# Side work of TensorE moved to common ticks in a two-block language model on one core

## What is computed

```python
# first block
x = x + mamba2_mixer(x, ...)        # 32 heads of 64 in 4 groups, state 128, chunks of 128 tokens
x = x + conv_ffn(x, ...)            # gate and up of 2816, 3-tap convolution, silu
k, v = shared_kv(x, ...)
x = x + diff_attention(x, k, v, ...)  # 8 heads, two softmaxes each, p0 - lam * p1
x = x + conv_ffn(x, ...)
# second block
h = rms_norm(x)
y_conv, y_fox, y_swa = ...          # short convolution; forgetting attention, 8 heads of 64;
                                    # window attention of 128 tokens with sinks, 8 heads, 2 kv heads
x = x + (g0 * (y_conv @ w0) + g1 * (y_fox @ w1) + g2 * (y_swa @ w2)) @ w_mix_out
x = x + cross_attention(rms_norm(x), rms_norm(mem), ...)   # 4 heads of 256, 256 memory tokens
x = x + swiglu(rms_norm(x), ...)
out = rms_norm(x)
```

## Time and profile before

| what | value |
|---|---|
| median of three runs | 2459.2 us (2458.94 to 2461.61) |
| profiled execution | 2459.41 us |
| its span, first to last instruction | 2457.6 us |
| TensorE busy | 2418.4 us, 98% |
| VectorE, ScalarE, POOL busy | 1398.4, 972.2, 406.3 us |
| DMA engines busy | 27.2% (weights), 2.0%, 0.3% by queue |
| mean granted clock of TensorE | 0.995 |

### The profile page before, as it was taken

How to read it: one execution, slowest core, us unless ns; L and a number is a source line. 1 busy time by engine, 2 the same in 40 slices (tenths; PEclk the granted TensorE clock), 3 DMA queues, 4 the chain that set the end, 5 groups by cost and what they waited for, 6 DMA issues and landing times.

```text
span 2457.6 us, 30359 instructions
## 1 busy us (share of the span) xinstructions
PE 2418.4 (98%) x11930; PEld 1963.1 (80%) x11930; DVE 1398.4 (57%) x2286; ACT 972.2 (40%) x1595; POOL 406.3 (17%) x320
## 2 busy tenths in 40 slices
PE   8899999999999999999999999999999999999998
PEld 6677777888888887878888887787788887888887
DVE  6878876663665445576546547534565445343342
ACT  5444434442344444454334434424443334322223
POOL 0352332220111222122002100001220101110011
PEclk9999999999999999999999999999999999999999
DMA  4532222223223221132232242231234322223222
GB/s 160 101 88 86 78 69 77 95 94 102 96 84 122 65 69 51 48 113 97 90 105 91 81 137 78 69 112 53 65 120 134 120 87 85 98 91 102 96 84 87
DMA packets 74269, 226.23 MB, mean 92 GB/s; under 512 B 8080, under 2 KB 12304, under 8 KB 74000
## 3 DMA queue, kind: packets, MB, share of 16 engines
q1 hardware_dynamic: 69696, 215.90, 27.2%
q10 hardware_dynamic: 4432, 8.39, 2.0%
HBM read 215.87 MB, written 8.39 MB: 91 GB/s over the span
## 4 chain that ended last, share of the span: by engine, by line
PE 59%; issue 0%; DVE 0%; ACT 0%; POOL 0%; POOLq 0%; DVEq 0%
PE bank L1142 58%; PE bank L1146 1%; ACT t L1536 0%; DVE t L1972 0%; DVE t L1979 0%; DVE t L1975 0%; ACT t L1539 0%; POOL t L2546 0%; POOLq L2767 0%; DVEq L2767 0%; DVE t L2468 0%; DVE t L2474 0%; POOLq L765 0%
## 5 line engine op out<-in xcount | busy, mean ns | idle before, releaser
L1142 PE MATMUL bank<-t 128*128 128x512 f32 (+4 forms) x11412 | 2388.0, 375 | 29.2 <-DVE t L1972 14.9
L1142 PEld LDWEIGHTS bank<-t 128*128 128x128 f32 (+1 forms) x11412 | 1907.7, 186 | 468.2 <-issue 85.3
L1536 ACT ACTIVATE t<-t 128x1024 fp32r<-128x1024 f32 (+5 forms) x649 | 549.3, 856 | 684.2 <-PE bank L1142 277.3
L1972 DVE TENSOR_TENSOR t<-t 128x1024 fp32r<-128x1024 f32 (+6 forms) x686 | 624.7, 921 | 251.4 <-ACT t L1536 246.4
L2546 POOL TENSOR_TENSOR t<-t 128x512 f32<-128x512 f32 (+5 forms) x240 | 365.7, 1530 | 1650.6 <-ACT t L1539 549.0
L1972 DVE TENSOR_TENSOR t<-bank,t 128x512 f32<-128x512 f32 (+4 forms) x410 | 275.6, 676 | 490.1 <-PE bank L1142 472.3
L1539 ACT ACTIVATE t<-t 128x512 f32<-128x512 f32 (+5 forms) x545 | 330.6, 616 | 536.9 <-DVE t L1972 328.1
L1975 DVE SCALAR_TENSOR_TENSOR t<-t 128x512 f32<-128x512 f32 (+6 forms) x430 | 321.1, 752 | 94.8 <-ACT t L1539 54.0
L1536 ACT ACTIVATE t<-bank 128x512 f32<-128x512 f32 (+4 forms) x150 | 71.5, 493 | 130.5 <-PE bank L1146 90.6
L2549 POOL TENSOR_SCALAR t<-t 128x128 f32<-128x128 f32 (+3 forms) x64 | 40.0, 630 | 389.0 <-ACT t L1536 252.7
L1146 PE MATMUL bank<-t 128*128 128x128 f32 x518 | 81.5, 275 | 2.1 <-ACT t L1536 1.0
(11 more groups left out here) (26 smaller groups left out, 60.1 us busy)
## 6 DMA issues: line engine op xcount, KB each, us to landing
t<-in_w SPq DMA_DIRECT2D x304, 512.0 KB, 3.4
t<-in_w SPq DMA_DIRECT2D x48, 384.0 KB, 3.0
t<-in_w SPq DMA_DIRECT2D x56, 320.0 KB, 2.9
t<-in_w SPq DMA_DIRECT2D x28, 256.0 KB, 3.2
tab<-t ACTq DMA_DIRECT2D x1, 2560.0 KB
t<-in_x SPq DMA_DIRECT2D x8, 256.0 KB, 5.6
t<-tab SPq DMA_DIRECT2D x8, 256.0 KB, 3.8
spill<-t ACTq DMA_DIRECT2D x1, 2048.0 KB, 8.2
```

The source lines that it names most:

```text
L1142: return eng.matmul(out, lhs, rhs, start=start, stop=stop, skip_group_check=loose)
L1536: return eng.activation(out, in_, ACT.Copy, scale=scale)
L1972: return eng.tensor_tensor(out, a, b, o)
```

## The change

Ages and starts are moved; no operation is added or taken away.

- Scan: value products at age 6 (was 5), follow-up at 7, POOL's addition at 8; gate at 9, next group's start at 7.
- Row norms of q and k start at even ticks only, row at age 6, a head at the earliest at age 8; heads start at even ticks only.
- Mixer: window attention's transposes at 4i + 8 and values at 4i + 12; forgetting attention's at 4i + 10 and 4i + 14, so that all steps of each fall into every fourth tick. What waits for them waits four ticks more.
- Cross attention: heads start at even ticks, both value products at age 14.

```diff
     def rms(self, key, g=1):
-        n = 4 if g == 1 else 5
+        n = 4 if g == 1 else 6
...
-            if self.when(name, key) is None and test() and self.place(windows):
+            if self.T % step == 0 and self.when(name, key) is None and test() and self.place(windows):
...
-                      and (g == 0 or self.past("pair", (g - 1, 3), 6)), [(("bt", g), 0, 2), (("scb", g), 0, 2)])
+                      and (g == 0 or self.past("pair", (g - 1, 3), 7)), [(("bt", g), 0, 2), (("scb", g), 0, 2)])
...
-                          [(("s0", g, p), 0, 3), (("s1", g, p), 0, 3), (("bo", g, p), 3, 2), (("by", g, p), 5, 2)])
-            self.once("gate", g, lambda g=g: self.past("pair", (g, 3), 8) and have([("z", g, i) for i in range(4)], 1))
+                          [(("s0", g, p), 0, 3), (("s1", g, p), 0, 3), (("bo", g, p), 3, 2), (("by", g, p), 6, 2)])
+            self.once("gate", g, lambda g=g: self.past("pair", (g, 3), 9) and have([("z", g, i) for i in range(4)], 1))
...
-            while want and want[0][1] <= self.T and all(self.T >= t + 3 for t in done[-3:-2]) and self.rms(want[0][0], 2):
+            while want and self.T % 2 == 0 and want[0][1] <= self.T and all(self.T >= t + 3 for t in done[-3:-2]) and self.rms(want[0][0], 2):
...
-        def normed(key, age=7):
+        def normed(key, age=8):
...
-                windows += [(("sqk", tile, i, 0), 4 * i, 2), (("sqk", tile, i, 1), 4 * i, 2), (("sat", tile, i), 4 * i + 6, 2)]
-            windows += [(("so", tile), 8, 15)]
+                windows += [(("sqk", tile, i, 0), 4 * i, 2), (("sqk", tile, i, 1), 4 * i, 2), (("sat", tile, i), 4 * i + 8, 2)]
+            windows += [(("so", tile), 12, 15)]
...
-                    windows += [(("fqk", tile, i, half), 4 * i + 2, 2), (("fat", tile, i, half), 4 * i + 8, 2)]
-            windows += [(("fo", tile), 10, 15)]
+                    windows += [(("fqk", tile, i, half), 4 * i + 2, 2), (("fat", tile, i, half), 4 * i + 10, 2)]
+            windows += [(("fo", tile), 14, 15)]
...
-            windows += [(("xo_", h, 0), 15, 3), (("xo_", h, 1), 16, 3)]
+            windows += [(("xo_", h, 0), 14, 3), (("xo_", h, 1), 14, 4)]
...
-        for g, p in at("pair", T - 5):
+        for g, p in at("pair", T - 6):
             bank = take(("by", g, p))
...
-            for tile in at("swa", T - 4 * i - 6):
+            for tile in at("swa", T - 4 * i - 8):
...
-            for tile in at("swa", T - 4 * i - 8):
+            for tile in at("swa", T - 4 * i - 12):
...
-            for tile in at("fox", T - 4 * i - 8):
+            for tile in at("fox", T - 4 * i - 10):
...
-            for tile in at("fox", T - 4 * i - 10):
+            for tile in at("fox", T - 4 * i - 14):
...
-            for h in at("xh", T - 15 - d):
+            for h in at("xh", T - 14):
                 bank = take(("xo_", h, d))
```

More of the change, by code:

```diff
@@ L338, in norm_rule, with once @@
         self.rules.append(rule)
-    def once(self, name, key, test, windows=()):
+    def once(self, name, key, test, windows=(), step=1):
         def rule():
-            if self.when(name, key) is None and test() and self.place(windows):
+            if self.T % step == 0 and self.when(name, key) is None and test() and self.place(windows):
                 self.start(name, key)
@@ L433, in group_in @@
                 if g >= 2:
-                    before, age = (("pair", (g - 2, 3)), 6) if i < 2 else (("yn", g - 2), 0)
+                    before, age = (("pair", (g - 2, 3)), 7) if i < 2 else (("yn", g - 2), 0)
                     self.until(lambda: self.past(*before, age), ("in", g, i))
@@ L521, in diff @@
                       and (h == 0 or self.past("head", h - 1, 8))
-                      and self.tok_begun.get(("v", h // 2), 1 << 30) <= self.T, windows)
+                      and self.tok_begun.get(("v", h // 2), 1 << 30) <= self.T, windows, 2)
             def o_norm(h=h):
@@ L614, in mix @@
             branch(0, c, "cv")
-        self.until(lambda: self.past("swa", 3, 22), "swa")
+        self.until(lambda: self.past("swa", 3, 26), "swa")
         for i in range(2):
@@ L625, in mix @@
             branch(2, c, "sw")
-        self.until(lambda: self.past("fox", 3, 24), "fox")
+        self.until(lambda: self.past("fox", 3, 28), "fox")
         self.start("mem", 0)
@@ L1514, in tensor_program @@
                 rms_row(key, 1)
-        for key in at("rms2", T - 5):
+        for key in at("rms2", T - 6):
             rms_row(key, 2)
@@ L1806, in mix @@
                         *sig["ex"].up("s", tile, i, half))
-            for tile in at("swa", T - 4 * i - 7):
+            for tile in at("swa", T - 4 * i - 9):
                 L = buf.Lm[(4 * tile + i) % 5]
@@ L1811, in mix @@
                 copy(two(L[:, :]), two(K.of(("sat", tile, i))[:, :])).then_inc(*leave(("sat", tile, i)))
-        for tile in at("swa", T - 21):
+        for tile in at("swa", T - 25):
             hi, _ = buf.operand("sw", tile)
@@ L1831, in mix @@
                         *sig["ex"].up("f", tile, i, half))
-            for tile in at("fox", T - 4 * i - 9):
+            for tile in at("fox", T - 4 * i - 11):
                 for half in range(2):
@@ L1836, in mix @@
                     copy(L[:, 0:n], K.of(("fat", tile, i, half))[:, 0:n]).then_inc(*leave(("fat", tile, i, half)))
-        for tile in at("fox", T - 23):
+        for tile in at("fox", T - 27):
             hi, _ = buf.operand("fo", tile)
@@ L1895, in cross @@
         for d in range(2):
-            for h in at("xh", T - 16 - d):
+            for h in at("xh", T - 15 - d):
                 hi, _ = buf.operand("ox", 2 * h + d)
@@ L2195, in ssm @@
                 t.then_inc(*sig["sub"].up(g, p, k))
-        for g, p in at("pair", T - 6):
+        for g, p in at("pair", T - 7):
             xs = buf.XS[g % 2][:, p, :]
@@ L2281, in diff @@
             ts(buf.l4[:, 5:6], buf.l4[:, 4:5], LAM_INIT, ADD).then_inc(*sig["lam"].up())
-        for key in at("rms2", T - 6):
+        for key in at("rms2", T - 7):
             dst = K.head_dst(key)
@@ L2388, in mix @@
                     ts(L[:, a], L[:, a], s8[:, 5:6], MUL).then_inc(*sig["pn"].up("s", tile, i, half))
-        for tile in at("swa", T - 22):
+        for tile in at("swa", T - 26):
             two_parts("sw", tile, K.of(("so", tile))[:, :]).then_inc(*leave(("so", tile)))
@@ L2412, in mix @@
                     ts(L[:, 0:n], L[:, 0:n], s8[:, 5:6], MUL).then_inc(*sig["pn"].up("f", tile, i, half))
-        for tile in at("fox", T - 24):
+        for tile in at("fox", T - 28):
             two_parts("fo", tile, K.of(("fo", tile))[:, :]).then_inc(*leave(("fo", tile)))
@@ L2477, in cross @@
         for d in range(2):
-            for h in at("xh", T - 17 - d):
+            for h in at("xh", T - 16 - d):
                 two_parts("ox", 2 * h + d, K.of(("xo_", h, d))[:, :]).then_inc(*leave(("xo_", h, d)))
@@ L2600, in ssm @@
                 tt(d[:, :], d[:, :], buf.cbm[:, :, :].rearrange("p c n -> p (c n)"), MUL).then_inc(*sig["gm"].up(g, p, k))
-        for g, p in at("pair", T - 7):
+        for g, p in at("pair", T - 8):
             xs = buf.XS[g % 2][:, p, :]
```

12 lines of the change are left out of this document (6 added, 6 removed).

## The result

The changed kernel takes 2480.62 us (median of 4 runs, 2479.88 to 2481.11) against 2459.07 (4 runs): ratio 1.0089, 95% interval 1.0076 to 1.0101. It is 21.6 us slower; the forecast was 4.8 us slower, with a range of 2456 to 2471 us.

The account below looks back on a forecast made before the run. TensorE was taken as the bound nearly everywhere. Scan +9.5, mixer +1.2, attention -4.9, cross attention -0.1, merges -1.9 and small new waits +1 gave +4.8 us: 2464.0 us, range 2456 to 2471.

Parts of the forecast that it names:

- The chain through follow-up, addition and exponentials: Scan: VectorE's follow-up, POOL's addition, then ScalarE's exponentials free the banks late; TensorE waits at each group's fourth pair.
- all three waits of the earlier trace: Differential attention: 1.7 us for logits banks, 0.8 for ScalarE's square, 1.0 at the output projection; 1.7, 0.8, 0.7 saved.
- 25 merges: Differential attention: about 25 full-array transpose blocks merge with others, each saving 0.025 us.
- the size of the scan, +9.5 us: Scan: 7.3 us from later banks, gate and norm, plus 2.2 us of slow clock, together +9.5 us.
- The clock, 2.2 us forecast: Scan: waits of about 3 us in groups 1 and 2 bring half-clock spells, costing 2.2 us (0 to 5.1).
- Attention -4.9: Differential attention: even ticks and later row norms remove waits and a 1.7 us half-clock loss, -4.9 us (0 to -5.2).
- Mixer +1.2 and its merges: Mixer: lost adjacent half-array pairs cost 3.2 us, ended waits return 2: +1.2; about 32 merged blocks save 0.025 us each.
- a relief of 2 and eight lost pairs (2.2): Forgetting attention: later transposes end waits inside blocks, saving 2 us; eight side-by-side half-array pairs go, 0.27 us each.
- Cross attention -0.1: Cross attention: an earlier second value product hides a 0.7 us wait, a 1.0 us ScalarE wait grows by 0.6: -0.1.
- slack in the scan: Rival, scan: POOL's addition comes before TensorE needs the banks; without the 9.5 us, 2454.5 us; chance 0.17.
- half waits: Rival, scan: waits half as long and no slow clock, so 9.5 falls to 3.7 us, 2458 us; chance 0.15.
- The absent relief: Rival, differential attention: VectorE and ScalarE hand over in bursts, three waits reappear, 2468.9 us; chance 0.18.

Follow-up runs that it names:

- rest_only: The change without its scan part (attention, mixer and cross attention only), against the kernel before: 2449.8 us, ratio 0.9965.
- slip: The kernel before, with group 1's pairs and gate held to the ticks they have in the changed kernel: 2463.8 us, ratio 1.0016.
- piece_first: The changed kernel with the projection piece issued ahead of the side work in the scan's ticks: 2468.4 us, ratio 1.0045 to the kernel before.
- rest_grouped: The change without its scan part, mixer blocks ordered as all transposes, then values, then logits: 2451.7 us, ratio 0.9971 to the kernel before.
- odd: The changed kernel with attention heads and their row norms at odd ticks instead of even: 2481.5 us, ratio 1.0096 to the kernel before.
- no_slip: The changed kernel with follow-up and value products first, plus another bank so group 1's fourth pair starts a tick earlier: 2458.9 us, 1.0000 of the kernel before.

## Why the prediction was wrong

**Right.** TensorE is the bound and the scan sets the sign. The chain through follow-up, addition and exponentials is the one that made groups 1 and 2 wait. Without the scan's part the heads lie where the forecast put them, and all three waits of the earlier trace rows are gone.

**Right by luck.** That stretch then gained 4.5 us, with 4.9 forecast as 3.2 of waits and 1.7 of slow clock. Measured in rest_only: waits fell by 2.3 us only (a new one of 1.6 us came at 815 us); the clock gave nothing, since a spell follows the new wait; and TensorE's own work shrank by 2.2 us, for which the forecast had only its 25 merges at 0.025 us, 0.6 us. What shortened that work was not tested.

**The step that failed: the size of the scan, +9.5 us, measured +27.3** (+24.7 at the median with the scan's part alone). By place, the measured column with slow clock, the forecast's without (its 2.2 us of clock had no place):

| place | forecast | measured |
|---|---|---|
| group 0 | +1.2 | +4.8 |
| group 1 | +3.1 | +4.8 |
| start of group 2 | 0 | +6.9 |
| group 2 | +1.5 | +7.8 |
| group 3 | +0.7 | +3.3 |
| last gate and norm | +0.8 | -0.3 |

Four causes of it:

- *The addition was taken at 1.0 us.* That is what it took in the earlier trace rows, as the last of a row of three POOL operations, and again there in the changed kernel (1.02 us); the mean of the sixteen was 1.2 already. It now starts when the follow-up ends, in group 2 beside VectorE's work on 1024 columns. The same group by form, before and after (busy us, mean ns, idle before):

```profile
L2546 POOL TENSOR_TENSOR t<-t 128x384 f32<-128x384 f32 x16 | 19.4, 1212 | 9.6 <-DVE t L1975 9.6
```
```profile
L2546 POOL TENSOR_TENSOR t<-t 128x384 f32<-128x384 f32 x16 | 29.2, 1825 | 35.5 <-DVE t L1975 35.5
```

  At group 2 it took 3.11 us. Less the 16.4 us by which the trace is late there, TensorE came at 255.6 (forecast 255.3), the addition began at 257.0 (256.5), and both banks were free at 261.2 (258.6): 2.1 of the 2.6 us are the addition's length.
- *Nothing was said on the start of group 2.* The forecast let pairs of group 1 slip a tick and priced the wait inside the group. The fourth pair slipped two ticks, as the norm's sum and row, the state and value products left it no two free banks at tick 83, and the gate three. The work fell among the convolutions of group 2, where VectorE has no idle time (busy 4.17 of the 4.20 us from 211.3): +3.6 us of wait and a 6.8 us spell. slip shows 2.6 us of the wait by itself, with a spell of 3.4 us.
- *The clock, 2.2 us forecast, some 9 measured.* The sum took 2.2 us, little more than one spell of 3.4 us. In the trace six waits of 2.1 to 5.1 us between 100 and 404 us have one each, five of them of 6.8 us and not the 3.4 of the earlier trace rows; a seventh, 2.5 us at 429.6, has none. The kernel before already had a spell of 6.8 us (at 372.7, among waits of 0.7, 2.05 and 1.2 us), which the forecast did not read. The upper bound of 5.1 us, half of three spells of 3.4, was too low as well.
- *The full tick itself.* Group 1's wait was forecast at the fourth pair; it came at the third's state products (3.3 us), which had the bank of that pair's own selection products and waited for the same exponentials. piece_first shows that most of it was VectorE standing idle behind the block, which the sum held only as TensorE's time. Group 3 had the same in small: 1.1 us at its third pair, for VectorE's subtractions, which nothing in the sum held, while the fourth pair, which the sum charged with 1.3 us, waited 0.35.

**Attention -4.9, measured -1.4 with the scan's part,** all of it the spell (waits 5.1 us against 4.5 before). The heads' even grid was worked out from the old start of the projections; the scan's extra tick moved these to odd ones. Steps of a change were priced as if independent.

**Mixer +1.2 and its merges, measured -1.9.** The 0.27 us of the earlier trace rows is right for halves side by side against apart, but not for halves with transposes between. Window attention, before and after, from the tick before its first step to the same projection:

```profile
1451.73:1589.32 137.59, 137.59 (x727) 105.25 (x727) 87.28 (x264) 61.70 (x154) 0.00 (x0) 1.00 0.22 71
```
```profile
1477.64:1615.23 137.59, 137.59 (x727) 105.71 (x726) 87.36 (x264) 60.84 (x154) 0.00 (x0) 1.00 0.23 71
```

Lost pairs and merges cancel to the hundredth. Four ticks with values, transposes and logits take 7.29 us so and 7.11 with the halves adjacent (rest_grouped): 0.18. And a transpose block put next to values alone costs 6.67 us for the four ticks, against 6.76 in the earlier trace rows apart: 0.09, not 0.025, beyond the forecast's bound of 0.05 and near the 0.1 that it named as a sign of being wrong. The drain at a change of mode that the Trainium skill names (TensorEngine Tiling (Array Packing), Key Properties) would have given 2.4 us of loss instead of 3.2; the windows above show a net of nothing, and no run isolates the drain. The forgetting attention gained 1.9 us, where a relief of 2 and eight lost pairs (2.2) were to cancel. Since the order alone gives 1.2 us back there (rest_grouped), I estimate relief and merges at some 3 us, more than forecast.

**Cross attention -0.1, measured -2.4.** Both waits there went (1.0 and 0.7 us); the forecast let the first grow by 0.6, and it did not.

The rivals: slack in the scan and half waits are refuted by the traces. The absent relief came true in the changed kernel, but by the shift of one tick and not by heads in bursts, as odd and rest_only show. None reached beyond 2471 us. The range failed since every bound of the scan was set term by term, with no case for a wait elsewhere.

**Left open.** How much of the last 1 us of the wait at tick 101 is due to POOL slowing VectorE and how much to the idle time before it: no_slip doesn't separate it, and piece_first, which takes 1.5 us off, moves both. Whether the long addition is due to VectorE's work beside it. And why TensorE's own work in the attention is 2 us shorter in rest_only and odd.

## What to carry to other kernels

Gathering one engine's work starves another whose in-order queue is headed by something behind the gathered block: look at who stands at the head of the other queues in a full tick, and put the piece that they wait for first. A consumer moved a tick later must be followed through buffers of two to whoever overwrites them, and the wait costs its slow clock too (9.1 us on top of 17.9 here); swapping two operations in one queue or a third buffer gave back 14.6 of 21.6 us. In a plan with even-tick grids and first-fit banks, price the parts together: one tick of shift undid 3 us of a gain elsewhere. And check each term of a sum, not only the total: the attention's 4.5 us came from other terms than the forecast's 4.9.

## What was unexpected of the hardware

The granted clock fell to 0.50 without any idle time in the trace. rest_grouped and rest_only at the same matmuls, a stretch with 16 records of products of one and two columns (start of head 5), then the next 3.4 us:

```profile
955.13:962.68 7.55, 7.55 (x50) 6.68 (x49) 4.01 (x10) 3.36 (x8) 2.22 (x2) 1.00 0.15 43
962.68:966.10 3.42, 3.42 (x11) 2.63 (x10) 0.19 (x1) 0.79 (x3) 0.39 (x1) 0.50 0.00 0
```
```profile
956.09:963.60 7.51, 7.51 (x50) 6.67 (x49) 4.02 (x10) 3.32 (x7) 2.18 (x2) 1.00 0.15 44
963.60:967.00 3.40, 3.40 (x19) 2.44 (x19) 1.52 (x4) 1.67 (x5) 0.43 (x1) 1.00 0.00 0
```

TensorE is busy throughout in both, with the same 50 records; one runs on at 1.2 GHz (11 records in 3.4 us), the other at 2.4 (19). The clock goes with the spread of one kernel: the 21 runs of the kernel before beside slip go from 2455.97 us at a mean clock of 0.996 to 2462.76 at 0.994. And POOL's addition of 384 columns took between 1.0 and 3.8 us, by what VectorE did beside it; the traces show the coincidence, no run isolated it.
